# Fewer columns of ones in the column sums of the modulation accumulators

## The reference, cut to what matters

```
mod   = silu(c_2) @ w_ada_2 + b_ada_2      # six parts of 2048: shift, scale, gate, twice
h     = rmsnorm(x) * (1 + scale1) + shift1 # ahead of the two attentions
...
h     = rmsnorm(x) * (1 + scale2) + shift2 # ahead of the feed-forward part
```

## Time and profile before

| | |
|---|---|
| runs | 1802.46, 1806.06, 1802.93 us |
| median | 1802.93 us |
| span of the profiled execution | 1802.5 us |
| granted TensorE clock, mean | 0.999 of full speed |
| TensorE busy, matmul rows | 1787.5 us of the span, 8394 records |
| TensorE busy, weight loads | 1470.4 us |
| VectorE, ScalarE, GpSimd busy | 1246.1, 906.1, 124.1 us |
| DMA | 427.01 MB, mean 237 GB/s |

### The profile page before, as it was taken

One profiled execution on the slowest core, in us unless ns is written; L12 is line 12 of the kernel. 1 busy time (PEld: TensorE's weight loads), 2 busy tenths in 40 slices (PEclk: granted clock), 3 DMA queues, 4 the chain that ended last, 5 costly groups with the idle time before them and its releaser, 6 DMA issues.

```text
span 1802.5 us, 25666 instructions
## 1 busy us (share of the span) xinstructions
PE 1787.5 (99%) x8394; PEld 1470.4 (82%) x8394; DVE 1246.1 (69%) x1669; ACT 906.1 (50%) x1289; POOL 124.1 (7%) x217
## 2 busy tenths in 40 slices
PE   9999999999999999999999999999999999999998
PEld 7777778887888888888888888888888888888886
DVE  5677779768877876777678767666665654544545
ACT  6766684545445454544445455444444444444443
POOL 1011101010000000210001101000000000000000
PEclk9999999999999999999999999999999999999999
DMA  9778779564777867798888957888876655555554
GB/s 357 254 254 284 246 255 335 178 212 149 227 225 230 264 210 263 241 307 286 286 284 278 314 180 257 255 254 254 254 232 185 184 184 193 194 192 192 194 191 140
DMA packets 181374, 427.01 MB, mean 237 GB/s; under 512 B 15568, under 2 KB 16064, under 8 KB 180928
## 3 DMA queue, kind: packets, MB, share of 16 engines
q1 hardware_dynamic: 152864, 322.30, 54.4%
q0 software_dynamic: 28304, 103.89, 18.0%
q10 hardware_dynamic: 144, 0.03, 0.0%
HBM read 424.07 MB, written 2.10 MB: 236 GB/s over the span
## 4 chain that ended last, share of the span: by engine, by line
PE 92%; DMA 3%; DVE 3%; ACT 1%; issue 1%; SPq 0%; DVEq 0%; ACTq 0%
PE bank L1921 29%; PE bank L1923 28%; PE bank L1922 28%; PE bank L1980 2%; DMA ada_raw<-in_w_ada 2%; DMA raw<-in_w_in_a 2%; DVE w_lo L1209 1%; PE bank L2131 1%; PE bank L2111 1%; DVE acc_a L1219 1%; PE bank L2248 0%; PE bank L2100 0%; PE bank L2255 0%; PE bank L2097 0%; DVE x L1247 0%
## 5 line engine op out<-in xcount | busy, mean ns | idle before, releaser
L1209 DVE TENSOR_TENSOR w_lo<-raw,w_hi 128x1024 fp32r<-128x1024 f32 x605 | 729.3, 1211 | 433.5 <-ACT w_hi L671 432.6
L671 ACT ACTIVATE w_hi<-raw 128x1024 fp32r<-128x1024 f32 x605 | 633.3, 1050 | 716.7 <-PE bank L1923 658.3
L1921 PE MATMUL bank<-w_hi,h_hi 128*128 128x512 f32 x2272 | 897.5, 395 | 3.0 <-DVE w_lo L1209 2.2
L1923 PE MATMUL bank<-w_hi,h_lo 128*128 128x512 f32 x2272 | 885.6, 390 | 0.0
L1922 PE MATMUL bank<-w_lo,h_hi 128*128 128x512 f32 x2272 | 884.7, 389 | 0.0
L1921 PEld LDWEIGHTS bank<-w_hi,h_hi 128*128 128x128 f32 x2272 | 426.9, 188 | 94.3 <-issue 6.6
L1923 PEld LDWEIGHTS bank<-w_hi,h_lo 128*128 128x128 f32 x2272 | 426.6, 188 | 90.2
L1922 PEld LDWEIGHTS bank<-w_lo,h_hi 128*128 128x128 f32 x2272 | 427.2, 188 | 85.0
L1219 DVE SCALAR_TENSOR_TENSOR acc_a<-ada_raw,cond,acc_a 128x1024 f32<-128x1024 f32 x112 | 143.2, 1279 | 13.3 <-DMA ada_raw<-in_w_ada 13.0
L575 POOL DMA_DIRECT2D ada_raw<-in_w_ada x160 | 84.7, 529 | 965.8 <-DVE acc_a L1219 718.8
L1219 DVE SCALAR_TENSOR_TENSOR acc_b<-ada_raw,cond,acc_b 128x1024 f32<-128x1024 f32 x48 | 64.3, 1339 | 2.0 <-DMA ada_raw<-in_w_ada 2.0
(11 more groups left out here) (209 smaller groups left out, 970.1 us busy)
## 6 DMA issues: line engine op xcount, KB each, us to landing
raw<-in_w_ff SPq DMA_DIRECT2D x256, 512.0 KB, 4.4
raw<-in_w_in SPq DMA_DIRECT2D x176, 512.0 KB, 4.6
ada_raw<-in_w_ada POOLq DMA_DIRECT2D x160, 512.0 KB, 4.9
raw<-in_w_in_a SPq DMA_DIRECT2D x69, 512.0 KB, 5.0
ada_more<-in_w_ada POOLq DMA_DIRECT2D x32, 512.0 KB, 6.1
raw<-in_w_out_a SPq DMA_DIRECT2D x32, 512.0 KB, 5.9
raw<-in_w_o SPq DMA_DIRECT2D x32, 512.0 KB, 5.3
raw<-in_w_moba SPq DMA_DIRECT2D x16, 512.0 KB, 4.7
```

Of the source, the lines that this page charges most:

```text
L671: act.activation(used(w_hi, turn, s), used(raw, turn, s), ACT.Copy).then_inc(hi_ready, 1)
L1209: dve.tensor_tensor(used(w_lo, turn, s), used(raw, turn, s), used(w_hi, turn, s).bitcast(F32), ALU.subtract).then_inc(lo_ready, 1)
L1921: pe.matmul(out_ap, hi, rhs_hi, start=start, stop=False)
L1923: return pe.matmul(out_ap, lo, rhs_hi, start=False, stop=stop)
```

## The change

Each sum multiplies by the first 16 columns of the tile of ones, and writes 16 columns of the bank, c to c + 15, in place of 128. The stationary tile, the order, the waits and the number of instructions are the same. (Blank lines that the diff also removes are left out.)

```diff
+        SUM_COLS = 16
...
-                    ins = pe.matmul(bank[:, c:c + P], acc[:, k * P:(k + 1) * P], ones, start=True, stop=True)
+                    ins = pe.matmul(bank[:, c:c + SUM_COLS], acc[:, k * P:(k + 1) * P], ones[:, 0:SUM_COLS],
+                                    start=True, stop=True)
```

## The result

The changed kernel takes 1811.35 us (median of 5, 1810.61 to 1813.17), the one before 1804.11 us (median of 5, 1802.46 to 1806.06). The ratio is 1.0044, with a 95% interval of 1.0033 to 1.0055: slower by 0.4%, small but clear of the noise; that is 7.2 us between the medians, 7.9 us by the ratio. It is the rival in which the clock falls in both rounds, and its price was higher than forecast: 1811.35 against 1808.3, and against 1806.5 at the upper end of the range.

The account below looks back on a forecast made before the run. TensorE, 92% of the chain that ended last, was taken as the bound. Only the turn's sums counted: 2 x 0.02 = 0.04 us off the 1802.5 span, plus 0.4 carried to the median, gave 1802.9 us; range 1800.3 to 1806.5.

Parts of the forecast that it names:

- the rival in which the clock falls in both rounds: TensorE's clock drops to 1.2 GHz around the sums, costing 2 x 2.7 = 5.4 us: 1808.3 us, chance 0.12.
- The step that the weight load sets the pitch: In all 128 sum records, loading the 128-column stationary tile takes 0.11 us, so narrower products leave the spacing near 0.1115 us.
- the turn: Place of each round's three sums, six records, with TensorE never waiting around them; 0.02 us saved a round, reaching the end.
- My 0.004 us saved for each record: Each sum record's spacing was to shrink from 0.1115 us towards the 0.107 us of a weight load.
- The rival in which columns set the pitch: Sum spacing falls with the columns moved; the three sums save 2 x 0.67 = 1.3 us: 1801.6 us, chance 0.16.
- the one with all 14.3 us on the path: Rival: the whole TensorE time of all 128 sum records comes off the end, giving 1788.6 us; chance 0.03.
- Which sums are hidden, and by what: Twelve behind VectorE's residual, seven behind the wait for the diagonal, ten behind unit 2's wait for h_lo; nothing saved on path.
- the ten sums: Last sums of a round, 20 records, delaying unit 0; 0.08 us saved there but taken back at unit 2's wait.
- the load as the floor with the clock unchanged: Main case: weight loads keep the sums' spacing and the clock stays at 1.00; 1802.9 us, chance 0.62.
- 0.77 us of idle in the stretch: TensorE pause between 346.29 and 356.10 us that left the clock at 1.00, taken as evidence against a clock fall.
- 3.0 of 9.8 us with columns moving, against 8.4: From 346.29 to 356.10 us, the time the array would move columns after the change, against now.
- 5.7 us at low clock for a round: Length of low-clock work at the trace's start, assumed to fall on the ten sums and after; 2.7 us lost a round.

Follow-up runs that it names:

- the seven rows of the table: Kernel before with 16, 32, 64, 72 or 96 columns in every sum, or 112 and 16 or 128 and 16 by turns: 1811.35 to 1802.85 us.
- the run with the last ten alone: Kernel before with 16 columns only in the last ten sums of each round, 128 in the others: 1806.12 against 1803.19 us, ratio 1.0013.
- the run of round 2: Kernel before with 16 columns in the 32 sums of round 2 only, 128 in round 1: 1807.96 against 1803.72 us, ratio 1.0020.

## Why the prediction was wrong

**What the sums cost: right.** The step that the weight load sets the pitch held to the hundredth: no gain in the turn, and the run with 256 columns shows the other side of the floor. My 0.004 us saved for each record were too much; the pitch stayed as it was. The Trainium skill's page "TensorE: Matmul & The Clock Gate" gives the load 107 ns (section "LDWEIGHTS"), and the trace agrees with 0.1115 us. The 25 ns that the Trainium skill gives in the same page's section "Back-to-back issue gap" were not seen here, where each product has a tile of its own to load; the section itself says that in a stream of loads and products both set the spacing. Here the measurement decides. The rival in which columns set the pitch is out, and so is the time of the one with all 14.3 us on the path. Which sums are hidden, and by what, was not tested: as the sums did not become shorter, the transposes, the product on the diagonal and the ten sums began at the same distances as before in any case.

**Which case is the likeliest: wrong.** I gave 0.62 to the load as the floor with the clock unchanged, and 0.12 to the fall in both rounds. The step that failed is the sentence against the fall: that weight loads go on without a pause, and that 0.77 us of idle in the stretch leave the clock alone. The runs show that the first half is no protection: in the seven rows of the table the loads are the same, and the clock falls in the four with 64 columns or fewer on the mean and not in the three with 72 or more. The idle proved nothing, because the sums around it moved 128 columns each. The working had the right number in it (3.0 of 9.8 us with columns moving, against 8.4) and I gave it 0.12 only. The Trainium skill, in the same page's section on the HAM clock gate, has the clock follow how busy TensorE has been; the trace has it fall to 0.50 behind a stretch in which TensorE counts as busy for 6.80 of 7.59 us, so the busy time that the profile counts did not tell it beforehand. That all five executions have a mean clock of 0.993 to 0.995 shows that it happens every time, in this kernel.

**The price: the mechanism right, the length too small.** I took 5.7 us at low clock for a round, from the start of the trace. It is about 10 us in the changed kernel. The ten sums cost 2.0 us more, as worked out (2.1). The rest of the low stretch, unit 0 and its four transposes, takes 364.26 - 358.29 = 5.97 us, where it took 359.30 - 356.10 = 3.20; 2.8 us are lost in place of my 0.6. With 2.0 + 2.8 and two rounds the rival would have stood at 1802.9 + 9.6 = 1812.5, and the range should have reached there. What unit 2 gives back (0.1) and the wait at 1042 us (0.8) are small against it.

**What stays open.** Why the clock falls at 349 us in one trace and at 356 in another, and how long it stays low (some 3 us in the run with the last ten alone, 7 with 64 columns, 10 in the changed kernel, over 13 in the run of round 2), was not taken apart; the experiments say in which stretch it falls and on what it hangs, not when exactly. Whether weight loads count for nothing at all was not tried; here they did not keep the clock. The number of columns moved and the time during which they move were changed together in every run, so the two are not told apart.

## What to carry to other kernels

Before a product is made narrower, look at the start of its stationary tile's load and at the next: if the two are a pitch apart, fewer columns gain nothing. And where TensorE has only small work for a while, here between two turns, the columns it moves may be what keeps its clock: making them fewer, in work most of which other engines hide, made this kernel 0.4% slower. Read the granted clock in windows of a few us around such places; busy time, and slices of 45 us, show nothing of it.

## What the runs showed of the hardware

- A plain float32 product with a fresh 128x128 stationary tile has a pitch of 0.112 us per record for 16 to 128 columns and of 0.216 us for 256; at 1.2 GHz the one with 16 columns has 0.214, and the one with 128 columns takes as long (ten sums in 4.43 and 4.44 us).
- With the same instructions at the same pitch, the time went by the columns moved in the whole stretch: 1807.28 and 1806.67 us for the two runs with a mean of 64 columns, 1802.85 and 1802.90 us for the two with a mean of 72. In the first two the granted clock fell to 0.50 and in the other two it stayed at 1.00. It is a result of this stretch with its own waits, and no rule for another.
- TensorE's busy time and its weight loads' were the same (6.80 and 6.51 us of 7.59, against 6.90 and 6.51) ahead of a fall of the clock and without one.
